# Eight of the 16 rounds of a top-128 choice moved from ahead of the attention into its first four steps

## The reference

```python
topk = min(TOPK_MAX, S // 4)                       # 128
rel = relu(einsum('bqhd,bsd->bqhs', q_idx, k_idx))
score = einsum('bqhs,bqh->bqs', rel, w_idx) * idx_scale
score = where(key_pos < chunk_limit(pos), score, NEG_INF)
_, sel = lax.top_k(score, topk)                    # the choice of keys, one for all heads
...
logits = einsum('bqhd,bqkhd->bhqk', q_a, k_a[sel]) * dh ** -0.5
o_a = softmax(logits) @ v_a[sel]                   # 8 heads of 64, "a"
...
o_b = chunk_causal_attention(q_b, k_b, v_b, pos)   # 8 heads of 96, "b", no choice
mixed = concatenate([o_a * silu(g_a), o_b * silu(g_b)])
h = h + mixed @ w_out
```

## Time and profile before

| what | us |
|---|---|
| median of 3 runs | 2756.62 (2755.81 to 2758.04) |
| time of the profiled execution | 2755.73 |
| its span | 2753.9 |
| TensorE busy | 2672.5 |
| VectorE busy | 1481.9 |
| ScalarE busy | 1134.4 |
| GpSimd busy | 1156.9 |

### The profile page before, as it was taken

How to read it: one execution, slowest core, us unless ns; L and a number is a source line. 1 busy time by engine, 2 the same in 40 slices (tenths; PEclk the granted TensorE clock), 3 DMA queues, 4 the chain that set the end, 5 groups by cost and what they waited for, 6 DMA issues and landing times.

```text
span 2753.9 us, 32761 instructions
## 1 busy us (share of the span) xinstructions
PE 2672.5 (97%) x13224; PEld 2149.7 (78%) x13224; DVE 1481.9 (54%) x2606; ACT 1134.4 (41%) x1556; POOL 1156.9 (42%) x864
## 2 busy tenths in 40 slices
PE   8987999999999999999999999999999999999997
PEld 7877677777888887777888886788888777788886
DVE  4599735557655135567555135575531565575522
ACT  4533834434433235654433235443332344433321
POOL 3344033335444543226445552354455332454452
PEclk9999999999999999999999999999999999999999
DMA  4224013213222331112223331223233322222232
GB/s 145 92 77 166 19 63 113 85 47 107 92 97 103 107 111 62 62 50 104 92 92 108 108 122 47 77 92 105 95 107 107 108 84 69 82 102 92 95 120 77
DMA packets 45607, 253.48 MB, mean 92 GB/s; under 512 B 4560, under 2 KB 9184, under 8 KB 17936
## 3 DMA queue, kind: packets, MB, share of 16 engines
q1 hardware_dynamic: 34656, 232.18, 24.1%
q10 hardware_dynamic: 10800, 19.20, 2.1%
HBM read 249.21 MB, written 10.55 MB: 94 GB/s over the span
## 4 chain that ended last, share of the span: by engine, by line
PE 83%; DVE 9%; ACT 3%; POOL 2%; issue 1%; DMA 1%; SPq 0%; DVEq 0%; ACTq 0%
PE ring L436 70%; PE ring L798 3%; POOL wlo L1000 2%; PE turn L803 2%; PE turn L436 1%; PE out L842 1%; PE ring L641 1%; DMA raw<-in_pieces 1%; DVE mask L1757 1%; DVE w L1754 1%; ACT whi L1049 1%; PE out L657 1%; PE out L886 1%; DVE sp L1937 1%; PE out L848 0%
## 5 line engine op out<-in xcount | busy, mean ns | idle before, releaser
L1000 POOL TENSOR_TENSOR wlo<-raw,whi 128x512 fp32r<-128x512 f32 x860 | 1156.7, 1377 | 1563.5 <-ACT whi L1049 1563.5
L436 PE MATMUL ring<-xh,whi 128*128 128x512 f32 x1880 | 752.1, 400 | 19.7 <-DVE gate L1720 9.4
L436 PE MATMUL ring<-xh,wlo 128*128 128x512 f32 x1880 | 734.8, 391 | 0.0
L436 PE MATMUL ring<-xl,whi 128*128 128x512 f32 x1880 | 734.5, 391 | 0.0
L1049 ACT ACTIVATE whi<-raw 128x2048 fp32r<-128x2048 f32 x215 | 411.4, 1914 | 430.5 <-DMA raw<-in_pieces 427.1
L436 PEld LDWEIGHTS ring<-xh,whi 128*128 128x128 f32 x1880 | 354.3, 188 | 125.6 <-issue 51.3
L436 PEld LDWEIGHTS ring<-xh,wlo 128*128 128x128 f32 x1880 | 354.2, 188 | 75.2
L436 PEld LDWEIGHTS ring<-xl,whi 128*128 128x128 f32 x1880 | 354.7, 189 | 73.0 <-issue 3.4
L2044 DVE SCALAR_TENSOR_TENSOR taps<-u,conv,taps 128x511 f32<-128x511 f32 (+1 forms) x344 | 295.9, 906 | 17.9 <-ACT taps L1442 15.6
L2058 DVE TENSOR_TENSOR u<-ring,r 128x512 f32<-128x512 f32 x168 | 114.5, 687 | 297.7 <-PE ring L436 297.7
L2034 DVE TENSOR_TENSOR h<-ring,h 128x512 f32<-128x512 f32 x72 | 49.6, 689 | 412.9 <-PE ring L724 376.4
(11 more groups left out here) (276 smaller groups left out, 3402.7 us busy)
## 6 DMA issues: line engine op xcount, KB each, us to landing
raw<-in_pieces SPq DMA_DIRECT2D x215, 1024.0 KB, 4.7
toep<-diag_store ACTq DMA_DIRECT2D x16, 512.0 KB, 3.6
diag_store<-diag_row ACTq DMA_DIRECT2D x1, 5120.0 KB, 23.5
band_store<-band_row ACTq DMA_DIRECT2D x1, 3072.0 KB, 31.3
h<-in_x SPq DMA_DIRECT2D x4, 512.0 KB, 6.5
wbias<-band_store ACTq DMA_DIRECT2D x4, 512.0 KB, 7.4
result<-h SPq DMA_DIRECT2D x8, 256.0 KB, 2.2
raw<-in_pieces SPq DMA_DIRECT2D x4, 256.0 KB, 6.7
```

Of the source, the lines that this page charges most:

```text
L436: ins = pe.matmul(out, stationary, moving, start=first and n == 0, stop=last and n == 2)
L1000: ins = pool.tensor_tensor(m.wlo[slot][:, part], m.raw[slot][:, part], m.whi[slot][:, part].bitcast(F32), ALU.subtract)
```

## The change

```diff
     def heads(b):
-        for t in range(8, 16):
-            pick_round(t)
-        make_mask()
         for k, (x, table) in enumerate(((m.k_a, m.turn_a[1]), (m.q_a, m.turn_a[0]))):
...
                 take_reciprocal(s, 1)
             if s + 1 < PAIRS:
                 take_prep(s + 1)
+            if s < PAIRS_B:
+                pick_round(8 + 2 * s)
+                pick_round(9 + 2 * s)
+            if s == PAIRS_B - 1:
+                make_mask()
             if 2 <= s < PAIRS + 2:
                 gate(s - 2)
```

## The result

The changed kernel takes **2781.88 us** (median, 2780.89 to 2783.52) against 2756.22 us beside it (2755.63 to 2758.04): a ratio of 1.009, 95% interval 1.0076 to 1.0105. The profiled execution took 2781.75 us. A second comparison, with more executions of the kernel before, gave 2782.06 against 2758.01 us, ratio 1.0088 (1.0072 to 1.0103), so the loss is about 24 us. The forecast was slower, 2770.9 us with a range of 2762.5 to 2778. The sign was right, the size was not: the true loss is over half as large again, and outside the range.

A forecast was written before the change was run, and what follows sets the result against it. VectorE was taken to bound the kernel before 260.84 us, its exchange with TensorE behind it. A delay of 8.6 us plus 6.6 us for the clock, on 2755.7, gave 2770.9 us, range 2762.5 to 2778.

The forecast's parts named there:

- Rival 4: In attn's four steps VectorE's idle time takes up the rounds, so not slower after all: 2758 us, chance 0.07.
- Part 2 without the clock: In attn, rounds and mask lengthen steps 0 to 3; with the front's gain, later steps start 8.6 us later.
- won by step 0's clock: In attn's step 0, scores at the higher clock level take 4.58 us instead of 7.30, winning 2.7 us.
- R of step 1: The moment VectorE takes the first score of attn's step 1: forecast 271.5 us, against 276.48 before.
- The term of the clock: In attn, TensorE idles under the rounds and its clock falls; steps 2, 3 and 4 pay 3 x 2.2 = 6.6 us.
- Rival 1: In attn the clock does not fall behind TensorE's idle stretches: 2764.3 us, chance 0.15.
- Rival 3: In steps 2 to 4 the lower clock lasts over TensorE's whole chain, costing 18.9 us: 2783 us, chance 0.08.
- Part 1, the front: In heads, removing 26.73 us of VectorE work brings the first copy and first score 10.6 us earlier.
- I take 250.2, as the middle of 247.4 and 253.3 is about the same: At the end of heads, VectorE's first copy of a head starts at 250.2 us, TensorE's transposes being the floor.
- Rival 2: In heads VectorE's norm and rope chain keeps its old durations, ending at 253.3; 3.1 us less gain: 2774 us, chance 0.10.
- The bullet on the root: In heads the keys' norm waits for ScalarE's reciprocal root, so it starts at about 216.5 us, 7.5 us earlier.
- Behind step 3 nothing differs: After attn's step 3 the steps follow TensorE and ScalarE as before; the 8.6 us delay goes through to the end.

The follow-up runs named there:

- ahead: The changed kernel with each step's two rounds placed ahead of the copies for the next pair instead of behind them; 2781.99 us, ratio 1.0084.
- half: Against the kernel before: four of the eight rounds stay in heads, the other four go one each into steps 0 to 3 of attn; 2761.33 us, ratio 1.0013.
- six_b: The kernel before with six rounds left in heads, two cut up over the scores of steps 0 and 1, mask in step 2; 2752.37 us, ratio 0.9981.
- filler: The changed kernel with 2, 4, 5 and 7 idle matmuls added on TensorE under the rounds in steps 1 to 4; 2770.04 us, ratio 1.004.
- a_early: The changed kernel with ScalarE's root for the keys moved ahead of its takes of q units 4 and 5; 2781.4 us, ratio 1.0082.
- the kernel before, again: The kernel before, unchanged, run once more for a second profile; 2758.73 us, ratio 1.0003.
- front_only: The kernel before with rounds 8 to 15 left out altogether, the mask still in heads and attn unchanged; 2750.6 us, ratio 0.9974.
- six_f: six_b with 4 and 3 idle matmuls added on TensorE ahead of the scores of steps 0 and 1; 2749.38 us, ratio 0.9965.
- b_fill: The kernel before with 13 and 3 idle matmuls added on TensorE ahead of the scores of steps 0 and 1; 2753.25 us, ratio 0.9982.

## Why the prediction was wrong, point by point

**Sign and mechanism inside attn: right.** The rounds stand between the copies and the scores, TensorE idles under them, the clock falls, and the front gives back far less than was put in. Rival 4 (VectorE's idle time takes the rounds up) fails for two rounds in a step, as "ahead" shows for either side of the copies; with one round in a step half and six_b come part of the way to it.

**Part 2 without the clock: right in steps 1 to 4.** The lengths 14.35, 16.4 and 16.0 were built by hand, 9.14 was the old one, and filler, in which the clock does not fall there, has 14.01, 16.52, 16.14 and 9.11. The length of step 0, 17.59 us for the forecast 17.7, came out right by luck. I let its scores run at full clock and ScalarE's issue of the bias rows hold the exponentials. But behind an idle stretch of 4.14 us the scores ran at the lower level, and they bound the step: the issue was over at 256.01 us, and from then on ScalarE waited for VectorE's maxima and these for the scores, which carry the chain from 253.96 us to the last of VectorE's takes. ScalarE's timeline and the chain:

```profile
256.07 0.40 ACT L1253 ACTIVATE e<-e,nmax 128x128 f32<-128x128 f32 x1 [7.12 <-DVE nmax L1773]
...
259.37 0.72 ACT L1253 ACTIVATE e<-e,nmax 128x512 f32<-128x512 f32 x1 [1.13 <-DVE nmax L1773]
```

```profile
253.96 7.37 PE ring L641 x16
```

So the 2.7 us "won by step 0's clock" were not won. That the length fits is because the front, too, came later than forecast, so the issue was over 1.2 us behind the first score and not about 3.7. With the 1.65 us by which this execution is early added, R of step 1 is 274.0, where the forecast had 271.5: 2.5 us late.

**The term of the clock: mis-sized, 9.3 instead of 6.6 us** (9.5 and 12.7 in two other executions). "3 x 2.2" failed in three ways. Step 1 was counted at nothing, hidden by the exponentials, and paid 1.6. The price of 2.2 was that of a fall under the scores alone; in steps 2 to 4 the level came back only within the products with v behind them, so the fall cost 2.4, 3.2 and 2.1. And the upper end that I set to the range from rows, 2.7 us for one fall, lay under the 3.2 of step 3 (3.9 in a_early). Rival 1 (no fall) fell with the windows at 0.50. Rival 3, whose 2783 us is near the result, is still wrong as a mechanism: behind the products the turns and transposes of the changed kernel take 1.31 and 0.60 us as at full clock, and its price would have been 18.9 us. By the Trainium skill's rule on transposes (TensorE: Matmul & The Clock Gate, "Part 4: PE-mode transpose") they do not count for the clock; no run here shows it lost over them, and in a_early it came back over them, so the measurement stands against the rule.

**Part 1, the front: 7.9 instead of 10.6 us.** The step that failed is "I take 250.2, as the middle of 247.4 and 253.3 is about the same". VectorE's chain was expected to be faster beside an idle GpSimd. Some of it was, but other parts ran beside GpSimd instead: the three small steps of q's norm took 3.1 us together where they had taken 0.6, and the last half of the rotation of q, which had run beside an idle GpSimd, took 8.1 us (243.04 to 251.18) where it had taken 3.9 (256.94 to 260.84). The first halves of the keys' and of q's rotation did win about 4 us each (4.9 for 9.0, 3.8 for 7.8). So the chain took 36.4 us, nearly its old 36.8. Rival 2, the late front at 253.3, is what happened: 214.80 + 36.4 = 251.2, and with the 1.65 us added 252.8. The bullet on the root was right, 214.80 + 1.65 = 216.45 for the forecast 216.5. a_early shows that it was incomplete: without the root the squares of q hold the chain.

**What the sum did not have: the step that took the time out of the range.** With the late R of step 1 and the clock corrected the sum is 8.6 + 2.5 + 9.3 = 20.4, the forecast 2776, and that is still inside the range. The lengths give the same 20.4 (19.5 between the two repeated executions, 338.04 - 318.55). What is left of the 24 us, about four (7.3 between the first two profiled executions), comes behind the changed code. "Behind step 3 nothing differs" was wrong. Four instructions of GpSimd that can be found in both traces, before and after, start at 381.91 and 402.12, 630.74 and 650.90, 1240.88 and 1263.92, 2400.99 and 2427.56 us: 20.2, 20.2, 23.0 and 26.6 us apart. The steps between these numbers are falls of the clock: one near 366 us, ahead of the first of them, one near 1243, and two more near 1680 and 2400 us. The first two, in the changed kernel:

```profile
365.96 3.78 PE L657 MATMUL out<-at,v_a 128*64 128x512 f32 x16 [1.61 <-ACT at L1266]
...
1243.63 2.40 PE L803 MATMUL turn<-ident,z 128*128 128x128 f32 x10 [3.18 <-DVE z L1942]
```

and in the kernel before:

```profile
347.27 2.38 PE L657 MATMUL out<-at,v_a 128*64 128x512 f32 x16 [1.62 <-ACT at L1266]
...
1223.42 1.31 PE L803 MATMUL turn<-ident,z 128*128 128x128 f32 x10 [3.15 <-DVE z L1940]
```

and the second place once more in the kernel before, again:

```profile
1223.27 2.39 PE L803 MATMUL turn<-ident,z 128*128 128x128 f32 x10 [3.14 <-DVE z L1940]
```

The same idle stretch, 1.61 and 1.62 or 3.18, 3.14 and 3.15 us, goes with a fall in one execution and with none in the other, at the second place even in two executions of the same kernel. Each such fall costs 1.4 to 3 us. There were three or four of them in the profiled executions of the change, none in the first of the kernel before and one in the second, and one to three in the other kernels. The Trainium skill (TensorE: Matmul & The Clock Gate, "What's actually happening") says of the start of a kernel that the number of slow matmuls differs from run to run of the same kernel; these rows agree with that for falls in the middle of one. Why the changed kernel should have more of them over many executions, or whether it has, **stays open**: shifting everything behind attn by 20 us may matter, but front_only and six_f, whose later steps come some 9 us earlier, had three and two such falls too, half had three, and b_fill, whose steps come 4 us earlier, one. Part of the first comparison is also a low draw of the kernel before: 2756.2 us there, 2757.9 to 2758.5 us over 15 to 21 executions in the later ones.

## What to carry to other kernels

Work that is taken off a chain wins only what the chain's next wait leaves: of 26.7 us VectorE idled 18.7 away, so six of the eight rounds could have stayed where they were at no cost (six_b, half). Idle time of an engine in a loop takes up little at a time: two whole rounds in each of four steps lengthened attn by 27 to 28 us, one in each by 7 to 8, one cut up in each of two by about 2. Before filling VectorE's gap, look at what it leaves TensorE with; where TensorE then idles a few microseconds in each turn, add the slow matmuls behind the stretch, up to the point where the row shows the clock back, or keep it busy with matmuls that nobody reads. And when a chain is freed of one wait, follow it to the next two before taking the gain: here the squares of q ended only 1.8 us before the chain reached them behind ScalarE's root, and GpSimd's work fell on other parts of the chain.

## What the runs showed of the hardware

- **Idle matmuls pay.** 18 of them under the rounds brought the change 12 us, 16 of them the kernel before 5.2 us. They delayed nothing in these places, where TensorE waited anyway: the first scores behind them start at 263.90 us in b_fill and 263.62 before.
- **Idle length does not decide a fall alone.** 0.88 and 1.47 us left the clock (half), 3.28, 4.10 and more lowered it in these steps, but 1.61 us went with a fall in one execution and 1.62 with none in another, and at another place 3.14 us lowered it in one execution of the kernel before and 3.15 left it at 1.0 in the other.
- **The clock came back over transposes alone** (a_early, 278.8 to 282.4 us), and was kept over them for 4.3 us in the kernel before.
- **Small VectorE products suffer most beside GpSimd.** A 128x32 product of two tiles (L1591) took 0.19 us with GpSimd idle and 1.22 beside its subtractions, 1.03 us more, as much as the 128x512 ones lose (0.69 to 1.78). MATCH_REPLACE8 of 128x512 stayed at 0.67 to 0.68 throughout, and so moving rounds away from beside GpSimd made none of them faster. The Trainium skill (GPSIMD Engine Reference, "1. Specifications") names contention for VectorE instructions with two SBUF inputs; these rows agree, and add that the loss is about a fixed 1.0 us, not a share: 1.23 became 2.20 for 128x1024 (L1579), and 2.29 became 3.31 for 128x2048 (L1602, in a_early).
